# The sum over the halves of the squares moves from VectorE to GpSimd in nine norms of a two-block model on one core

## What is computed

```python
def rms_norm(x, g):
    xf = x.astype(jnp.float32)
    y = xf * lax.rsqrt(jnp.mean(xf * xf, axis=-1, keepdims=True) + EPS)
    return (y * g.astype(jnp.float32)).astype(x.dtype)

def first_block(x, p, ...):
    for i in range(DEPTH):
        x = x + 0.5 * swiglu(rms_norm(x, ln_ffn1[i]), ffn1_w_gu[i], ffn1_w_down[i])
        h = rms_norm(x, ln_mix[i])
        ...
        x = x + 0.5 * swiglu(rms_norm(x, ln_ffn2[i]), ffn2_w_gu[i], ffn2_w_down[i])
        gate = jax.nn.sigmoid(rms_norm(x, ln_ple[i]) @ ple_w_gate[i])
        x = x + gate * (p[i] @ ple_w_in[i])
    return x
```

## Time and profile before

| | us |
|---|---|
| median of 3 runs | 1724.54 |
| lowest and highest of them | 1723.46, 1726.7 |
| the profiled execution, its own time | 1727.66 |
| its span, from the first to the last instruction | 1725.6 |
| PE busy in the span | 1671.9 |
| DVE busy | 1288.8 |
| ACT busy | 995.5 |
| GpSimd busy | 5.9 |

### The profile page before, as it was taken

The page is one execution under the profiler, slowest core; times in us unless marked ns, Lnnn a source line. Parts: engine busy times, 40 slices in busy tenths (PEclk is TensorE's granted clock), DMA queues, the critical chain, the costliest instruction groups (busy, mean ns, idle before and its releaser), DMA issues.

```text
span 1725.6 us, 37786 instructions
## 1 busy us (share of the span) xinstructions
PE 1671.9 (97%) x14502; PEld 1553.2 (90%) x14502; DVE 1288.8 (75%) x2137; ACT 995.5 (58%) x1562; POOL 5.9 (0%) x21
## 2 busy tenths in 40 slices
PE   7999999999999999999999999989999998899998
PEld 7999999899999989998989999989999998798887
DVE  6777877768777887776868777877887774567676
ACT  6544576445454664546565454678878875345544
POOL 0000000000000000000000000000000000000000
PEclk9999999999999999999999999999999999999999
DMA  6565543125555455555435555545555540145654
GB/s 240 187 190 182 171 135 123 51 83 180 189 189 192 160 173 192 183 184 161 143 108 181 190 186 185 170 158 178 182 191 175 181 148 4 52 149 181 194 185 144
DMA packets 75865, 278.21 MB, mean 161 GB/s; under 512 B 8433, under 2 KB 8689, under 8 KB 75249
## 3 DMA queue, kind: packets, MB, share of 16 engines
q1 hardware_dynamic: 75168, 273.54, 48.7%
q0 software_dynamic: 592, 3.15, 0.5%
HBM read 274.56 MB, written 2.10 MB: 160 GB/s over the span
## 4 chain that ended last, share of the span: by engine, by line
PE 84%; DVE 8%; ACT 5%; issue 2%; DMA 0%; SPq 0%; DVEq 0%; ACTq 0%
PE ps L484 83%; DVE w_lo L473 2%; ACT w_hi L465 1%; PE ps L2507 1%; DVE x L972 1%; DVE h L577 1%; ACT arena L2169 0%; DVE rstd L626 0%; DMA x<-x_t 0%; DVE arena L675 0%; ACT h L569 0%; ACT arena L591 0%; DVE a_lo L960 0%; DVE arena L917 0%; DVE h_of_feed_forward L577 0%
## 5 line engine op out<-in xcount | busy, mean ns | idle before, releaser
L484 PE MATMUL ps<-h,w_hi 128*128 128x256 f32 (+1 forms) x3380 | 722.1, 304 | 0.0
L473 DVE TENSOR_TENSOR w_lo<-raw,w_hi 128x1024 fp32r<-128x1024 f32 x514 | 621.5, 1214 | 79.9 <-ACT w_hi L465 60.6
L465 ACT ACTIVATE w_hi<-raw 128x1024 fp32r<-128x1024 f32 x514 | 539.2, 1050 | 216.3 <-PE ps L484 196.6
L484 PE MATMUL ps<-h,w_lo 128*128 128x256 f32 x2026 | 577.3, 286 | 23.0 <-DVE w_lo L473 15.7
L484 PEld LDWEIGHTS ps<-h,w_hi 128*128 128x128 f32 x3380 | 544.9, 190 | 26.5
L484 PEld LDWEIGHTS ps<-h,w_lo 128*128 128x128 f32 x2026 | 384.3, 190 | 29.9 <-DVE w_lo L473 14.5
L484 PE MATMUL ps<-h_of_feed_forward,w_hi 128*128 128x512 f32 (+1 forms) x1088 | 351.4, 374 | 0.0
L484 PE MATMUL ps<-h_of_feed_forward,w_lo 128*128 128x256 f32 x1000 | 278.4, 281 | 0.8 <-issue 0.6
L912 ACT ACTIVATE arena<-ps 128x256 f32<-128x256 f32 x208 | 79.9, 384 | 271.9 <-PE ps L484 271.9
L484 PEld LDWEIGHTS ps<-h_of_feed_forward,w_hi 128*128 128x128 f32 x1088 | 198.1, 188 | 36.5
L484 PE MATMUL ps<-a_hi,w_lo 128*128 128x256 f32 x776 | 217.8, 281 | 0.8 <-DVE a_lo L960 0.8
(11 more groups left out here) (370 smaller groups left out, 1441.4 us busy)
## 6 DMA issues: line engine op xcount, KB each, us to landing
raw<-weights SPq DMA_DIRECT2D x514, 512.0 KB, 3.4
con<-shape_constants SPq DMA_DIRECT2D x1, 1584.5 KB, 10.5
x<-x_t SPq DMA_DIRECT2D x1, 1024.0 KB, 5.0
stored<-x POOLq DMA_DIRECT2D x1, 1024.0 KB, 5.0
x<-stored POOLq DMA_DIRECT2D x1, 1024.0 KB, 7.8
out_t<-arena SPq DMA_DIRECT2D x4, 256.0 KB, 2.1
arena<-p_t POOLq DMA_DIRECT2D x2, 256.0 KB, 4.3
arena<-final_gain POOLq DMA_DIRECT2D x1, 512.0 KB, 4.5
```

Of the source, the lines that this page charges most:

```text
L465: A.activation(w_hi[:, u % RING, 0:n], raw[:, u % RING, 0:n], ACT.Copy).then_inc(s_hi, 1)
L473: V.tensor_tensor(w_lo[:, u % RING, 0:n], raw[:, u % RING, 0:n], f(w_hi[:, u % RING, 0:n]), SUB)\
L484: return TE.matmul(o, lhsT, rhs, start=start, stop=stop, skip_group_check=True)
```

## The change

The nine folds are taken off DVE's program and written into GpSimd's. GpSimd's list of DMAs becomes a loop over the stages, so that each fold stands between the DMAs where its stage comes; the waits and the semaphore that a fold raises stay the same.

```diff
@@ late_dve
             dve_split(dve, unit_base[stages[n]] + 2)
-            dve.wait_ge(s_sq, sq_at[n] + 2)
-            V.tensor_tensor(whole[:, 0:4, :], whole[:, 0:4, :], whole[:, 4:8, :], ADD).then_inc(s_fold, 1)
             if stages[n] == "odd":
@@ gpsimd
-            for s, n in n_ple.items():
-                if order[s] > 1:
-                    pool.wait_ge(s_x, 4 * (order[s] - 1))
-                pool.dma_start(pin, a_p[:, int(s[3]), :, :]).then_inc(s_pin, 16)
-            if "second" in stages:
-                mixers["second"][3](pool)
+            for n, s in enumerate(stages):
+                if s in n_ple and n > 1:
+                    pool.wait_ge(s_x, 4 * (n - 1))
+                if s in n_ple:
+                    pool.dma_start(pin, a_p[:, int(s[3]), :, :]).then_inc(s_pin, 16)
+                if s == "second":
+                    mixers["second"][3](pool)
+                if late[n]:
+                    pool.wait_ge(s_sq, sq_at[n] + 2)
+                    nc.gpsimd.tensor_tensor(whole[:, 0:4, :], whole[:, 0:4, :], whole[:, 4:8, :], ADD).then_inc(s_fold, 1)
             pool.wait_ge(s_x, 4 * order["mlp"])
             pool.dma_start(gain, a_gain).then_inc(s_gain, 16)
```

## The result

The changed kernel took 1730.7 us (median of 10 runs) where the kernel before took 1726.75 (10 runs): a ratio of 1.0025, with a 95% interval of 1.0017 to 1.0034, or some 4.3 us slower. The forecast of 1727.3 us missed, and with 1724.8 to 1730.6 the range just missed too.

The account below looks back on a forecast made before the run. PE, busy 97% of the span, was taken to bound the kernel. Lateness of PE's sum in ffn1, ffn2, ffn3, even and odd summed to +2.73 us on 1724.54, giving 1727.3 us, range 1724.8 to 1730.6.

Parts of the forecast that it names:

- The level: Whole kernel: the forecast's base was the median of three runs before the change, 1724.54 us.
- The addition on GpSimd: Each fold on GpSimd was to take 2.38 us, between two streams (1.90) and three (2.85).
- The handoffs: ACT's square to fold 0.17 us, fold to PE's sum 0.05; the sum could start 2.60 us after the squares.
- ffn1, ffn2, ffn3: Feed-forward openings: PE's sum late beyond its allowance, less idle given back, costing 1.01, 0.82 and 0.72 us.
- mlp: Opening of mlp: sum 0.58 us late, but PE's later idle of 0.94 for `a_lo` absorbs it, so 0.
- even and odd: Openings with the fold queued behind a split: earlier start offsets the slower engine, leaving +0.12 and +0.06 us.
- The rival: Blocked read path: GpSimd's fold and DVE's splits cannot read at once in even and odd; 1728.3 to 1729.5 us, chance 0.38.
- The sign: Blocked path in even and odd: fold or split lasts 2 us or more beyond its others, or starts where the other ends.
- ple0, ple1, ffn0: Openings where the later sum stays inside the allowance (4.01 us in ple0), so cost 0.
- the allowance: At each opening, time from the end of the squares until PE's sum is due; 1.3 to 4.0 us.
- The moved DMAs: GpSimd's DMAs of `p` and the gain go some microseconds later behind a fold; read only later, costed at nothing.
- the slow case: GpSimd's addition takes 2.85 us and its handoff 0.30; +6.0 us, 1730.5 us, chance 0.06.

Follow-up runs that it names:

- e1: The changed kernel with the folds of even and odd back on DVE, seven staying on GpSimd: 1730.82 us beside 1727.79 before, ratio 1.0015.
- e3: The changed kernel, but in even and odd DVE's split of the third unit waits for GpSimd's fold to end: 1730.94 us beside 1727.79 before, ratio 1.0016.
- e2: The changed kernel with only the folds of even and odd on GpSimd, seven back on DVE: 1729.95 us beside 1727.79 before, ratio 1.0012.
- e6: The kernel before, all folds on DVE, but in even and odd the fold ahead of the third unit's split: 1726.89 us beside 1727.79, ratio 0.9991.
- e7: The same kernel as e6 measured a second time against the kernel before: 1726.14 us beside 1726.91, ratio 0.9997.
- e4: The changed kernel with a GpSimd multiply of tiles 0 to 3 by one ahead of each fold: 1764.46 us beside 1726.89 before, ratio 1.0226.
- e8: The changed kernel, unaltered, measured a second time against the kernel before: 1733.26 us beside 1726.91, ratio 1.0036.

## Why the prediction was wrong, point by point

- **The level.** The sum was put on a median of three runs, 1724.54. Ten runs gave 1726.75, and 35 runs in another comparison 1727.79. Some 2.2 of the 3.4 us between forecast and measurement are this; the three runs shown spread over 3.2 us, and a base known no better than that needed a wider range. Against its own base the forecast was +2.7, and the measurement +4.3; the rest of the miss is the terms below.
- **The addition on GpSimd.** Forecast 2.38 us, as the middle between two and three streams; measured 2.38 to 2.40 where no split is running as it starts. That the middle came out to the hundredth is luck. The handoffs were 0.08 and 0.05 where 0.17 and 0.05 were taken, so that the sum starts 2.51 us after the squares for 2.60. The estimate of 2.25 us from "GPSIMD Engine Reference" (§ Performance versus the Vector engine of the Trainium skill) was 0.13 short.
- **ffn1, ffn2, ffn3.** Forecast 1.01, 0.82, 0.72, in all 2.55. Measured from the squares to the first down product, after against before: ffn1 1.03, ffn2 0.56 (e1), ffn3 0.57. The last two were mis-sized, since the idle ahead of `a_lo` gives back 0.63 and 0.41 and not the 0.47 and 0.35 of its bracket. The working for ffn2 also has PE's sum end near 615.4, where its own numbers give 611.18 + 2.60 + 1.99 = 615.77; the conclusion stands, since the reciprocal starts 5.37 us after the squares in e1 and 5.38 before. For ffn3 these rows of after answer, where the way from the sum to the first down product was 7.80 us and is now 7.39:

```profile
912.25 2.38 POOL L3438 TENSOR_TENSOR arena<-arena 128x1024 f32<-128x1024 f32 x1 [106.69 <-ACT arena L591]
...
914.69 1.99 PE L484 MATMUL ps<-arena,con 128*128 128x256 f32 x8 [0.81 <-POOL arena L3438]
...
922.08 0.28 PE L484 MATMUL ps<-a_hi,w_lo 128*128 128x256 f32 x1
```

- **mlp.** Forecast 0; measured some 0.15. The idle ahead of the first down product took most of it, as said (0.48 is left of 0.94):

```profile
1545.04 1.99 PE L484 MATMUL ps<-arena,con 128*128 128x256 f32 x8 [0.29 <-POOL arena L3438]
...
1551.08 0.50 PE L484 MATMUL ps<-w_hi,a_lo 128*128 128x512 f32 x1 [0.48 <-DVE a_lo L958]
```

- **even and odd: the step that failed.** Forecast 0.12 and 0.06, measured 1.08 and 1.06. "What the earlier start gives, the slower engine takes" left out that the earlier start puts the fold beside a split. The rival had the mechanism, the place and the price (1.15, and 1.24 if the split is first); it got 0.38 and the forecast 0.50, on the ground that no row showed GpSimd reading SBUF. That is no evidence against a shared path, and no row spoke for the two running side by side either, so that the forecast had no ground to stand above the rival. The sign that it gave for a blocked path, a duration of 2 us or more beyond the others, was too large: a fold held up by one split of 1.22 us grew by 1.05 and 1.08, a split held up by the fold by 0.16 to 0.9. The page "SBUF — State Buffer" of the Trainium skill (§ Who interferes with whom) had named it; the traces agree with the wait of the second for the first, by 3.44 against 2.38 us for the fold, and 3.25 against 2.36 for two splits behind it.
- **ple0, ple1, ffn0.** Forecast 0 inside the allowance, blocked or not: no wait of PE is left to see there in the profile of the change, with folds of 3.2 to 3.5 us. ffn0 is near the edge: in e3 PE came earlier and waited 0.34 us.
- **The sum of the parts.** 1.03 + 0.56 + 0.57 + 0.15 + 1.08 + 1.06 = 4.45 us by the traces, 4.3 by the ratio. Against the forecast's 2.73 even and odd add 1.96, ffn1 and mlp 0.17, and ffn2 and ffn3 take off 0.41. The two halves measured alone gave 2.6 (e1) and 2.1 (e2).
- **The moved DMAs** were costed at nothing. The trace of after bears that out for the two of `p`: they are issued at 394.60 and 914.58, take 3.0 us to land, and DVE first reads their data at 573.07 and 1093.07 (L479). No run shows what their traffic alone does to the weight loads.
- **The chances.** 0.15, 0.33 and the slow case's 0.06 make 0.54 for slower by over 0.2%, not the 0.49 that is given.

## What to carry to other kernels

An engine that is idle all day is still no free place for work: ask what reads the same memory at the moment when the moved work will run, since moving it off a queue can bring it beside the very instruction that it stood behind. First try whether a change of order on the same engine gives the gain; here, by the traces of e6 and e7, the fold ahead of the split takes away PE's whole wait ahead of the sum without a slower engine. And a change worth a few microseconds is to be forecast as a difference, on a base of more than three runs.

## What the runs showed of the hardware

- A blocked instruction does not show as idle: its own row is longer (GpSimd's fold 3.44 for 2.38 us, DVE's split 1.75 for 1.22). It grows by 0.1 to 0.2 us less than what was left of the other (0.94 left and 0.82 longer in ple0, 1.26 and 1.08 in odd). And the row that starts first by the trace need not be the one that goes first (in odd the fold's record starts 0.04 us ahead of the split's, and it waited).
- An instruction of DVE with one operand in PSUM and one in SBUF runs beside GpSimd's addition with no loss on either side (0.42 and 2.39 us in ffn1).
- GpSimd multiplies 128x1024 by a repeated column in 1.90 us (e4, ffn1), where adding two full tiles takes 2.38.
- PE's idle can cost more than its length. In e4 the matmuls behind six waits of 2.2 to 4.6 us ran at 1.2 GHz for a while, and a lateness of 18 us became some 32. The length of the wait alone does not decide it: behind 1.96 us in e4 and 1.85 in odd after the change the granted clock stayed at 1.00, behind 1.88 in odd of e8 it fell (0.79 from 804 to 812 us).
